# Expert weights in the ring: units of whole matrices with one transfer of 8192 B rows each, in place of half matrices with two transfers of 4096 B rows

## What is computed

```python
def swiglu(x, wg, wu, wd):
    return (jax.nn.silu(x @ wg) * (x @ wu)) @ wd
...
    # N_EXPERTS 64, TOP_K 8, D_EXPERT 256: each token goes to 8 experts
    def step(acc, inp):
        tok, wt, e = inp
        y = swiglu(x_pad[tok], w_gate[e], w_up[e], w_down[e]).astype(F32) * wt[:, None]
        return acc.at[tok].add(y), None
...
    y = routed_experts(xf, idx, w, w_gate, w_up, w_down) + swiglu(xf, ws_gate, ws_up, ws_down).astype(F32)
```

## Time and profile before

| | us |
|---|---|
| median of 3 runs | 2486.87 (2485.6 to 2488.68) |
| the profiled execution, its own time | 2478.74 |
| its span | 2476.9 |
| PE busy | 2217.3 (90%) |
| DVE busy | 1603.3 (65%) |
| ACT busy | 1258.7 (51%) |
| POOL busy | 467.6 (19%) |
| q1, share of 16 engines over the span | 49.7% |

### The profile page before, as it was taken

How to read it: one execution, slowest core, us unless ns; L and a number is a source line. 1 busy time by engine, 2 the same in 40 slices (tenths; PEclk the granted TensorE clock), 3 DMA queues, 4 the chain that set the end, 5 groups by cost and what they waited for, 6 DMA issues and landing times. The chain is left out here.

```text
span 2476.9 us, 36356 instructions
## 1 busy us (share of the span) xinstructions
PE 2217.3 (90%) x10361; PEld 1687.7 (68%) x10361; DVE 1603.3 (65%) x2559; ACT 1258.7 (51%) x2072; POOL 467.6 (19%) x337
## 2 busy tenths in 40 slices
PE   7989688987889999999999399998899999999992
PEld 6867667776657776777766265576577766777771
DVE  3759655446468887788777321533677777888883
ACT  3332112212237777777777112322377776877871
POOL 0000323230003322232322000000023232222320
PEclk9999899998799999999999699797999999999996
DMA  5221000000449999999998502015399999999993
GB/s 187 97 74 39 18 1 1 1 1 19 171 162 377 372 362 359 358 369 370 365 350 306 171 26 68 1 39 171 133 377 337 362 357 339 371 365 375 372 349 97
DMA packets 177844, 536.68 MB, mean 217 GB/s; under 512 B 25856, under 2 KB 55520, under 8 KB 177632
## 3 DMA queue, kind: packets, MB, share of 16 engines
q1 hardware_dynamic: 148720, 461.69, 49.7%
q0 software_dynamic: 25248, 69.25, 11.1%
q10 hardware_dynamic: 3792, 4.65, 0.5%
HBM read 501.56 MB, written 54.07 MB: 224 GB/s over the span
## 5 line engine op out<-in xcount | busy, mean ns | idle before, releaser
L1263 DVE TENSOR_TENSOR gu_l<-ring,gu_h 128x1024 fp32r<-128x1024 f32 x512 | 610.9, 1220 | 98.0 <-ACT gu_h L1149 91.0
L1149 ACT CAST gu_h<-ring 128x1024 fp32r<-128x1024 f32 x512 | 524.1, 1061 | 90.0 <-DMA ring<-in_moe_w_up 67.6
L1087 PE MATMUL bank<-gu_h,xgT_l 128*128 128x512 f32 x1024 | 413.3, 404 | 0.0
L1089 PE MATMUL bank<-gu_h,xgT_h 128*128 128x512 f32 x1024 | 401.9, 392 | 0.0
L1088 PE MATMUL bank<-gu_l,xgT_h 128*128 128x512 f32 x1024 | 400.8, 391 | 0.0
L1394 POOL DMA_INDIRECT xg<-h_rows,list_idx x128 | 146.8, 1147 | 1193.8 <-issue 773.4
L1412 POOL DMA_INDIRECT moe_sum<-y,out_idx x128 | 227.5, 1777 | 321.1 <-issue 300.0
L1120 PE MATMUL bank<-ring,hmT_f 128*128 128x512 f32 x544 | 279.9, 596 | 0.0
L1156 ACT CAST down_h<-ring 128x1024 fp32r<-128x1024 f32 x130 | 136.2, 1048 | 210.1 <-PE bank L1120 116.7
L1269 DVE TENSOR_TENSOR down_l<-ring,down_h 128x1024 fp32r<-128x1024 f32 x130 | 159.2, 1225 | 119.3 <-ACT down_h L1156 117.7
L1089 PEld LDWEIGHTS bank<-gu_h,xgT_h 128*128 128x128 f32 x1024 | 193.3, 189 | 42.9
(11 more groups left out here) (300 smaller groups left out, 3548.0 us busy)
## 6 DMA issues: line engine op xcount, KB each, us to landing
ring<-in_moe_w_gate SPq DMA_DIRECT2D x256, 512.0 KB
ring<-in_moe_w_up SPq DMA_DIRECT2D x256, 512.0 KB
ring<-in_moe_w_down SPq DMA_DIRECT2D x256, 512.0 KB
ring<-in_a_w_in SPq DMA_DIRECT2D x32, 512.0 KB
ring<-in_a_w_out SPq DMA_DIRECT2D x8, 512.0 KB
h_rows<-y SPq DMA_DIRECT2D x8, 512.0 KB, 2.7
moe_sum<-y ACTq DMA_DIRECT2D x8, 512.0 KB, 6.6
ring<-moe_sum SPq DMA_DIRECT2D x8, 512.0 KB, 6.3
```

What stands on the lines that cost most here:

```text
L1087: nc.tensor.matmul(out, lhsT=xl, rhs=wh, start=k == 0, stop=False)
L1089: last = nc.tensor.matmul(out, lhsT=xh, rhs=wh, start=False, stop=k == KD - 1)
L1149: nc.scalar.copy(gu_h[:, c, :, :], gate_up_cols(gate_slot, c * CH // 2, CH // 2)).then_inc(gu_hi.sem, 1)
L1263: nc.vector.tensor_tensor(gu_l[:, c, :, :], gate_up_cols(gate_slot, c * CH // 2, CH // 2), gu_h[:, c, :, :].bitcast(F32), ALU.subtract).th ...
```

## The change

The first two units of an expert are now whole matrices, gate and up. Each of an expert's three units is filled by one transfer of 128 rows of 8192 B: three transfers of 1 MB in place of six of 512 KB. The shared expert's gate and up become whole units too, but are still loaded by two transfers of 4096 B rows each. `slot_loaded` counts 16 per filling of an expert's unit (`arrival`). Since a chunk needs a piece of both matrices, ACT waits for both units ahead of chunk 0, and both slots come free with the last chunk, where the first came free with chunk 1.

```diff
-            for j in range(2):
-                half = slice(j * HALF, (j + 1) * HALF)
-                add_unit((gate[:, half], up[:, half]), None, gu_ready, gu_shared, next_slot())
+            for w in (gate, up):
+                add_unit(w, None, gu_ready, gu_shared, next_slot())
...
-                add_unit(None, None, gu_lo, gu + CH_GU * e + CH_GU // 2, slots[0])
+                add_unit(None, None, gu_lo, gu + CH_GU * (e + 1), slots[0])
                 add_unit(None, None, gu_lo, gu + CH_GU * (e + 1), slots[1])
...
+        def arrival(n):
+
+            return LOADED if units[n][0] is not None else LOADED // 2
...
-                j, c0 = divmod(c0, HALF)
-                return ring[:, slot + j, :].rearrange("p (g c) -> p g c", g=2)[:, :, c0:c0 + width]
+                return ring[:, slot:slot + 2, c0:c0 + width]
...
-                    if c % 2 == 0:
-                        arrived(act, c // 2)
+                    if c == 0:
+                        arrived(act, 0)
+                        arrived(act, 1)
...
-                        for h in range(2):
-
-                            w, c0 = (weights[h], j * HALF) if j < 2 else (weights[2], h * HALF)
-                            sp.dma_start(ring[:, slot_of(n), h * HALF:(h + 1) * HALF], w[bass.ds(r + 4 * i, 1), :, c0:c0 + HALF].rearrange("e p c -> (e p) c")).then_inc(slot_loaded[slot_of(n)].sem, 16)
+                        sp.dma_start(ring[:, slot_of(n), :], weights[j][bass.ds(r + 4 * i, 1), :, :].rearrange("e p c -> (e p) c")).then_inc(slot_loaded[slot_of(n)].sem, 16)
```

More of the change, by code:

```diff
@@ L255, in loaded @@
             slot, turn_no, _ = place[n]
-            done = sum(1 for m in in_slot[slot][:turn_no] if not isinstance(m, tuple))
-            return slot_loaded[slot].sem, LOADED * (done + 1)
+            return slot_loaded[slot].sem, sum(arrival(m) for m in in_slot[slot][:turn_no + 1] if not isinstance(m, tuple))
+        def arrival(n):
+            return LOADED if units[n][0] is not None else LOADED // 2
         def unit_cols(n):
@@ L273, in load_units @@
                     sp.wait_ge(used.sem, value)
-                if isinstance(view, tuple):
-                    parts = [(ring[:, slot_of(n), j * HALF:(j + 1) * HALF], view[j]) for j in range(2)]
-                elif width:
+                if width:
                     dst, k = unit_cols(n), view.shape[1] // 2
@@ L1020, in arrived @@
                     arrivals, value = loaded(n0 + j)
-                    eng.wait_ge(arrivals, value + LOADED * i)
+                    eng.wait_ge(arrivals, value + arrival(n0 + j) * i)
                 return slot_of(n0), slot_of(n0 + 2), arrived
             def gate_up_cols(slot, c0, width):
-                j, c0 = divmod(c0, HALF)
-                return ring[:, slot + j, :].rearrange("p (g c) -> p g c", g=2)[:, :, c0:c0 + width]
+                return ring[:, slot:slot + 2, c0:c0 + width]
             def bump(pool):
```

## The result

The changed kernel takes 2538.18 us (2533.81 to 2542.56, 4 runs) against 2487.64 us of the kernel before (2485.6 to 2488.68, 4 runs). The ratio is 1.0204, with a 95% interval of 1.0183 to 1.0226: 50 us or 2% slower. The forecast was 2528 us. Medians in this document are over all executions, and the ratios leave out one execution of early_after and one of two_by_64 that fell in a slower state of the chip. The profiled span grew from 2476.9 to 2532.0 us, by 55.1 us.

A forecast was written before the change was run, and what follows sets the result against it. The DMA engines were taken to bound the kernel at 10.14 us a step, the chain of stores nearly as long. Stores setting the step until the ring fills: +28 - 7.5, +21 per stage, +41 on 2486.87: 2528 us, range 2455 to 2620.

The forecast's parts named there:

- the chain of stores: POOL's stores to `moe_sum`, each issued once the one before has landed, go from 9.59 to 12.6 us and set the step.
- The transfers themselves: Weight loads in the expert stages: longer rows cost 2% less engine time, -0.15 us a step (bounds +0.08 to -0.40).
- ACT's wait for both matrices: Silu starts 2.1 us later in a step, paid once as lead of the loads: 0 to 2.5 us per stage.
- Rows ahead of a store, +2.5 us: Weight rows served before a POOL store's first row: if a number of rows, they last twice as long, +2.5 us.
- my own list of signs: Signs in the profile after; a store's first q0 record 5 us after issue ended means right, still 3 us the first rival.
- the first rival: The engines win: what stands ahead of a store is bytes, or engines cut rows; 2473 us (2437 to 2482), chance 0.34.
- Turns, +0.5 us: Each q0 record of a store may wait longer between q1's rows: 0 to 1.7 us, 0.5 taken.
- a full ring: Once the weight ring is full, SP is held by slots, q1 runs empty between loads, and stores find fewer rows ahead.
- Eleven dear steps, then back to the engines' pace: Per expert stage, 11.5 steps 2.5 us longer until the ring is full (+28 us), then 50 steps at -0.15 (-7.5).
- the need of 9.98 us: Time a step needs of the DMA engines after the change, down from 10.14 us.
- the high end: Freed slots' loads stand ahead of each store: half of the 124 steps stay at +2.5, +155, 2642 us; includes late gathers.

The follow-up runs named there:

- early_after: The changed kernel with DVE's copies of the two lists moved from the end of its step to behind hmT_l, some 6 us earlier: 2516.85 us.
- two_by_64: The changed kernel with each matrix loaded by two transfers of 64 partitions each, rows still of 8192 B: 3147.67 us.
- early_two_sums: The changed kernel with stores of even and odd experts in two chains to two sums, and DVE's lists copied early: 2487.04 us.
- rows4096: The changed kernel, units still whole matrices, with each matrix loaded by two transfers of column halves in 4096 B rows: 2494.25 us.

## Why the prediction was right, step by step

The sign, the place (the expert stages), the carrier (the chain of stores) and nearly the size (2528 against 2538.18, with +41 against +48.5 us in the stages) came out. The sum reached it with terms of which two were wrong in opposite senses, so that the forecast came within 10 us is in part luck.

- **The transfers themselves: right.** Forecast -0.15 us a step of engine time. Measured 500.9 to 486.3 us and 501.7 to 490.1 us over 62 steps: -0.24 and -0.19. It is not seen in the time because the engines no longer set it; in early_two_sums, where they do, the stages are 12.7 us shorter than before, which fits.
- **ACT's wait for both matrices: right in this kernel.** 0 to 2.5 us per stage were allowed, and ACT has no such wait. Where the engines set the pace, in rows4096, the waits for gate and up double (60.6 and 67.5 us), but those for down go; in time it is at most 9 us for both stages. The prediction read only the waits for gate and up and left out those for down, 60.2 us in the same stage.
- **Rows ahead of a store, +2.5 us: the step that failed.** I took what stands ahead of a store's first record to be a number of rows. It is a number of bytes. After the change the store of 1018.87 leaves POOL at 1021.06:

```profile
1018.87 2.19 POOL L1412 DMA_INDIRECT moe_sum<-y,out_idx  x1 [7.03 <-issue]
...
q1 hardware_dynamic: 125, 0.95, 88.9%
...
q1 hardware_dynamic: 16, 0.13, 63.9%
q0 software_dynamic: 8, 0.03, 34.3%
```

The second line is 1021.06 to 1024: q1 alone, some 8 records per engine where the earlier trace rows has 20 in the same time. The last two are 1024.0 to 1024.5, where q0 appears: 3 us after the issue ended, not 5. Counted over all 122 stores of the two stages, the median from the end of the instruction to the first row of q0 is 3.0 us before and 3.0 us after; ahead of it each engine starts 15 rows of 4096 B (62 KB) or 7 rows of 8192 B (58 KB). Beside rows of 2048 B it is 2.7 us, 23 rows and 47 KB. Nor is it a fixed time: in two_by_64, where a byte takes the engines longer, it is 5.1 us for 7.6 rows, again 62 KB (97 stores). By my own list of signs this spoke for the first rival; the term was 0.
- **Turns, +0.5 us: right in kind, undersized.** The bounds were 0 to 1.7. It measured +0.86 us for a store's rows and +0.60 us for a gather's; the gather's share I had not put into a term at all.
- **The chain of stores: right, and shorter than forecast.** Forecast 12.6 us. After the change four stores in a row, from 1051.32 to 1095.41, take 11.02 us each, where the earlier trace rows has 9.59:

```profile
1051.32 2.27 POOL L1412 DMA_INDIRECT moe_sum<-y,out_idx  x1 [8.18 <-issue]
...
1062.51 1.44 POOL L1412 DMA_INDIRECT moe_sum<-y,out_idx  x1 [7.65 <-issue]
...
1095.41 1.88 POOL L1412 DMA_INDIRECT moe_sum<-y,out_idx  x1 [8.65 <-issue]
```

  Those four lie further apart than most. Over all 122 stores the time from a store's issue to the end of its last row went from 7.8 to 8.3 us on average, and the next store is issued 2.1 us (before) or 2.2 us (after) behind that, at the median. So the chain ran as long as the step in both kernels, more closely than the prediction had it, and its +0.5 us is about the +0.39 us by which a step grew. It is less than the +0.86 us of the rows because 32 of the 122 stores, against 7 before, had their first row within 1.5 us; in some of these cases q1 had run empty, as the forecast had it for a full ring, in others the cause stays open.

- **Eleven dear steps, then back to the engines' pace: failed, in the other sense.** The ring did fill (SP waits 522.8 us for slots), but the step did not fall back to the need of 9.98 us: the mean steps of the two stages are 10.32 and 10.72 us, for a full ring does not put a gather forward. The wait passed from ACT's weights to PE's gathered rows (61 waits, has one of the kernel before), through both stages. I named gathers only as room for the high end; they are the main path. Leaving that out and taking 2.5 us too many for the rows ahead nearly cancelled. The ring was also fuller before than I said: in the second stage, which the earlier trace rows leaves out, SP already waited 25 times, 41.4 us in all, for the slots of down:

```profile
SPq L1453 <- PE bank L1120: 41.4, 25, 4.0
```

## What to carry to other kernels

The length of a row is a choice between two queues. The DMA engines take the rows of different queues in turns. So in this kernel rows of 8192 B in the large queue were a little cheaper per byte (40.5 against 41.8 us of engine time per MB) and made each small transfer beside them longer (a store's rows 4.04 against 3.18 us). Look for the chain of small dependent transfers (here the accumulating stores, and the gathers queued behind them in the same program) and compare its length with the step before rows are made longer. Where a saturated resource becomes unsaturated while the time grows, as the DMA engines here (1.00 to 0.93 in the second stage), something else has become the bottleneck; here it was such a chain.

## What the runs showed of the hardware

- What a store of POOL finds ahead of it goes by bytes, not by rows or time: per engine 23 rows of 2048 B (47 KB), 15 of 4096 B (62 KB) or 7 of 8192 B (58 KB) in 2.7 to 3.0 us, and 7.6 rows of 8192 B (62 KB) in 5.1 us where the engines were slower (two_by_64).
- Rows of 2048 B beside a store cost it hardly less than those of 4096 B (3.03 and 3.18 us for 64 rows), those of 8192 B much more (4.04).
- Two transfers to 64 partitions each need 64.0 us of engine time per MB in place of 40.5 for one to all 128, and made the kernel 26% slower.
- After 3.54 us of idle time PE's matmuls took up to twice their time for 3.5 us, at a granted clock of 0.79 in the 6 us from there; most waits had no such price (39 of 45 of 0.5 us or more).
